# Two matmuls of 256 tokens in place of one of 512 in the weight-slot products of a hybrid transformer stack

## The chip, the cores and the metric

The kernel runs on one core of one Trainium2 chip. The metric is the device time of one execution in microseconds (us), taken as the median over the runs. The names of the engines are those of the profile: PE is TensorE's matmuls, PEld its weight loads, DVE is VectorE, ACT is ScalarE, POOL is GpSimd, and SP is SyncE, which issues the DMAs.

## The reference, cut to what matters

One block of mixed attention and convolution is followed by four layers of another block (mLSTM, sliding-window attention, HGRN2, differential attention). There are 512 tokens, the model width is 1024, the hidden width of every feed-forward part is 2816, and everything is in float32. What the change touches is the dense products: the input projections, the output projections and the feed-forward matrices.

```python
x = x + groups @ w_out
h2 = rms_norm(x, g_ffn)
return x + (jax.nn.silu(h2 @ w_gate) * (h2 @ w_up)) @ w_down      # first block
...
gu = h @ w_in                                                      # layers 0 to 3
return (jax.nn.silu(gu[..., :FFN_HIDDEN]) * gu[..., FFN_HIDDEN:]) @ w_out
```

## The kernel before, in words

Activations lie feature-major in SBUF: 128 features on the partitions, the 512 tokens along the free axis, so an activation of width 1024 is 8 chunks of 128x512, and the hidden one of width 2816 is 22. Each float32 product is made of three products of the one-pass format fp32r: the weight and the activation are each split into a high and a low part, and high x high, high x low and low x high are added in PSUM. The parts are `w_hi`, `w_lo`, `h_hi`, `h_lo`, `hid_hi` and `hid_lo`.

The weights come as a stream of 501 slots of 128x1024 values (512 KB). SP loads a slot into one of four buffers `raw`, ACT copies it to `w_hi` (L1440), POOL subtracts to `w_lo` (L623), and PE uses it. A slot is eight 128x128 weight blocks.

On PE a slot is used in one of several ways:

- `slot_products` (from L750), called by `m_tile`, takes the weights as the stationary operand and moves 128x512 activations past them. For each of the slot's blocks it issues three matmuls, L756, L757 and L758, all into one bank of PSUM, 128 outputs by 512 tokens. L756 and L757 have the same weights `w_hi`. One tile of a projection of width 1024 is one slot (24 matmuls); one of the down projection is three slots with 8, 8 and 6 blocks. Each call begins with a wait for the slot's low part (L752). `linear` calls `m_tile` in a loop of four tiles, so of 96 matmuls, wherever at least four tiles are left; `residual_tiles` calls it for the output and down projections without a loop.
- `early_chunk` (L854, L855, L859) does the first three tiles after a norm chunk by chunk, `gate_piece` (L1258 to L1260) does the output gates of two layers, and `value_slot` (L808 to L810) and `value_tile` (L825 to L827) make token-major values with the activations as the stationary operand. `mlstm_gates` (L1245 to L1247) and the compressed blocks of the first part (L1153) are small products of the same format. None of these is touched.

Each matmul call becomes two instructions, a weight load (LDWEIGHTS, PEld) and a MATMUL (PE). The banks are read out by ACT and DVE, whose signals `lin_free` let PE reuse one of four banks.

Of the kernel before, what the change touches and what calls it, by code (L numbers as in the profile page):

```python
# [218 lines left out]
def program(nc, xT, wstream, ada, cond, cols, kept, bigc, layerc, pos, yT, parts):  # L219
    slots_total = stream_length(parts)  # L220
    ctx = ExitStack()
    with ctx:
# [4 lines left out]
        def place(name, shape, dt, at=None):  # L227
            size = int(np.prod(shape[1:]))
            if at is None:
                at = top[0]  # L230
                top[0] += -(-size // 8) * 8
            return nc.alloc_sbuf_tensor_at(name, shape, dt, offset=base + 4 * at)
# [9 lines left out]
        w_hi = [place(f"w_hi{r}", [P, 8, P], F32R) for r in range(RING)]  # L242
        w_lo = [place(f"w_lo{r}", [P, 8, P], F32R) for r in range(RING)]
# [68 lines left out]
        for lv in range(7):  # L312
            b, at = 2 << lv, big + 40 * S if lv == 0 else ada_at + 2048 - (4096 >> lv)
# [432 lines left out]
        def _(pe):  # L746
            n = Counts()
            mm, turn = nc.tensor.matmul, nc.tensor.transpose

            def slot_products(k, i, step, pairs, first, last):  # L750

                pe.wait_ge(sm.lo_done, k + 1 + step * i)  # L752
                r = k % RING
                for at, (out, w, hi, lo) in enumerate(pairs):
                    begin, end = first and w == 0, last and w == len(pairs) - 1
                    mm(out, w_hi[r][:, at, :], hi, start=first and at == 0, stop=False)  # L756
                    mm(out, w_hi[r][:, at, :], lo, start=False, stop=False)  # L757
                    op = mm(out, w_lo[r][:, at, :], hi, start=False, stop=last and at == len(pairs) - 1)  # L758
                op.then_inc(sm.slot_used, 1)

            def m_tile(k, mt, i, step, mt_step, hi, lo, chunks, parts_from=None):

                if mt >= 4:
                    pe.wait_ge(sm.lin_free, mt - 3 + mt_step * i)
                c0 = 0
                for s, m in enumerate(chunks):
                    if parts_from is not None:
                        pe.wait_ge(sm.part_lo, parts_from + c0 + m)
                    slot_products(k + s, i, step,
                                  [(bank[mt % 4][:, 0:hi.shape[2]], c, hi[:, c0 + c, :], lo[:, c0 + c, :])  # L770
                                   for c in range(m)], s == 0, s == len(chunks) - 1)
                    c0 += m
# [2052 lines left out]
```

## Time and profile before

| | before |
|---|---|
| median of 2 runs | 3290.38 us (3289.63 to 3291.13) |
| span of the profiled execution | 3288.7 us |
| PE busy | 3220.8 us, 98% |
| PEld busy | 2619.6 us, 80% |
| DVE, ACT, POOL busy | 1549.8, 1202.1, 1480.9 us |
| matmuls, and as many weight loads | 15181 |
| HBM traffic | 114 GB/s over the span |

The span is the time from the first to the last instruction of one execution. PE's busy time is the union of its matmuls, which overlap: a matmul's record runs until its results are written, while the next has started long before. What one matmul costs in a stream is therefore the distance between two starts, not its duration. The profile was taken on the only core.

### The profile page before, as it was taken

Reading aid. Unit: us, or ns where it says so; the run is one execution under the profiler, and the core shown is the slowest. Engines: PE = TensorE matmul, PEld = TensorE weight load, DVE = VectorE, ACT = ScalarE, POOL = GpSimd, SP = SyncE. Lnnn points to the kernel's source line nnn. Section 1 sums busy time; section 2 is a strip of 40 time slices with the busy share of each in tenths; the row PEclk is TensorE's granted clock in tenths of the full one; section 3 lists DMA queues with packets and bytes.
Section 4 is the critical chain, followed back from the end, with each engine's and each line's share of the span. In section 5 each row is a group of like instructions: output and inputs, shape, how many; then the busy total and the mean of one; then the engine's idle time right before and its main releaser. Section 6 shows DMA issues by size and latency. Waiting matters only on the chain.

```text
span 3288.7 us, 42736 instructions
## 1 busy us (share of the span) xinstructions
PE 3220.8 (98%) x15181; PEld 2619.6 (80%) x15181; DVE 1549.8 (47%) x2615; ACT 1202.1 (37%) x1875; POOL 1480.9 (45%) x724
## 2 busy tenths in 40 slices
PE   8999999999999999999999999999999999999998
PEld 6876788888778888887888878877888877788886
DVE  2453355501145555467555224656556354752223
ACT  3455333222335332455432243125332243553322
POOL 3540554454235445524544454446444453154442
PEclk9999999999999999999999999999999999999999
DMA  4400155532224554211556333113555322032331
GB/s 161 122 26 1 65 204 191 202 106 93 68 65 160 193 202 145 84 59 63 180 191 208 105 96 96 39 33 103 204 191 188 103 90 77 5 99 96 96 103 64
DMA packets 103107, 376.12 MB, mean 114 GB/s; under 512 B 11456, under 2 KB 11584, under 8 KB 102848
## 3 DMA queue, kind: packets, MB, share of 16 engines
q1 hardware_dynamic: 102816, 373.86, 34.1%
q8 instruction: 81, 1.33, 0.2%
q0 software_dynamic: 160, 0.52, 0.1%
q14 instruction: 50, 0.41, 0.0%
HBM read 372.24 MB, written 2.10 MB: 114 GB/s over the span
## 4 chain that ended last, share of the span: by engine, by line
PE 52%; DVE 2%; ACT 1%; issue 1%; POOL 0%; DVEq 0%; ACTq 0%
PE bank L758 13%; PE bank L757 13%; PE bank L756 13%; PE bank L1362 2%; PE bank L859 1%; PE bank L854 1%; PE bank L855 1%; PE bank L808 1%; PE bank L809 1%; PE bank L810 1%; PE bank L1072 1%; PE bank L1328 1%; PE bank L1089 0%; PE bank L974 0%; PE bank L1258 0%
## 5 line engine op out<-in xcount | busy, mean ns | idle before, releaser
L623 POOL TENSOR_TENSOR w_lo<-raw,w_hi 128x1024 fp32r<-128x1024 f32 x501 | 1227.3, 2455 | 1368.2 <-ACT w_hi L1440 1368.0
L1440 ACT ACTIVATE w_hi<-raw 128x1024 fp32r<-128x1024 f32 x501 | 526.8, 1057 | 1183.2 <-PE bank L758 1022.4
L756 PE MATMUL bank<-h_hi,w_hi 128*128 128x512 f32 x2280 | 889.3, 390 | 0.0
L758 PE MATMUL bank<-h_hi,w_lo 128*128 128x512 f32 x2280 | 887.1, 389 | 0.0
L757 PE MATMUL bank<-h_lo,w_hi 128*128 128x512 f32 x2280 | 887.0, 389 | 0.0
L756 PEld LDWEIGHTS bank<-h_hi,w_hi 128*128 128x128 f32 x2280 | 427.9, 188 | 90.6 <-issue 2.0
L757 PEld LDWEIGHTS bank<-h_lo,w_hi 128*128 128x128 f32 x2280 | 427.9, 188 | 89.7 <-issue 1.0
L758 PEld LDWEIGHTS bank<-h_hi,w_lo 128*128 128x128 f32 x2280 | 427.9, 188 | 89.2
L2608 DVE CUSTOM_DVE_ANT_0 ada_raw<-ada_raw,cond_row 128x1024 f32<-128x1024 f32 x192 | 304.2, 1587 | 280.5 <-DMA ada_raw<-ada 270.6
L756 PE MATMUL bank<-hid_hi,w_hi 128*128 128x512 f32 x880 | 344.0, 391 | 0.0
L758 PE MATMUL bank<-hid_hi,w_lo 128*128 128x512 f32 x880 | 342.4, 389 | 0.0
L757 PE MATMUL bank<-hid_lo,w_hi 128*128 128x512 f32 x880 | 342.4, 389 | 0.0
L2624 DVE TENSOR_TENSOR hid_lo<-layer_const,hid_hi 128x512 f32 (+1 forms) x110 | 228.0, 2073 | 108.5 <-ACT hid_hi L1805 108.5
L661 POOL TENSOR_TENSOR h_lo<-proj,h_hi 128x512 fp32r<-128x512 f32 x40 | 55.7, 1407 | 308.5 <-ACT h_hi L1472 308.5
L757 PEld LDWEIGHTS bank<-hid_lo,w_hi 128*128 128x128 f32 x880 | 165.2, 188 | 35.3 <-issue 1.0
L756 PEld LDWEIGHTS bank<-hid_hi,w_hi 128*128 128x128 f32 x880 | 165.2, 188 | 35.1 <-issue 1.0
L758 PEld LDWEIGHTS bank<-hid_hi,w_lo 128*128 128x128 f32 x880 | 165.2, 188 | 34.3
L1800 ACT ACTIVATE layer_const<-bank 128x512 f32<-128x512 f32 x110 | 65.7, 597 | 321.1 <-PE bank L758 317.0
L2062 DVE SCALAR_TENSOR_TENSOR x<-bank,mod,x 128x512 f32<-128x512 f32 x64 | 48.0, 750 | 264.4 <-PE bank L758 255.7
L2621 DVE TENSOR_TENSOR layer_const<-bank,layer_const 128x512 f32<-128x512 f32 x110 | 75.9, 690 | 201.0 <-PE bank L758 163.4
L854 PE MATMUL bank<-h_hi,w_hi 128*128 128x512 f32 x336 | 135.5, 403 | 1.3 <-ACT h_hi L1472 1.0
L855 PE MATMUL bank<-h_hi,w_lo 128*128 128x512 f32 x336 | 131.9, 393 | 0.0
(411 smaller groups left out, 4016.5 us busy)
## 6 DMA issues: line engine op xcount, KB each, us to landing
raw<-weights SPq DMA_DIRECT2D x501, 512.0 KB, 3.5
ada_raw<-ada SPq DMA_DIRECT2D x192, 512.0 KB, 4.3
layer_const<-layer_const SPq DMA_DIRECT2D x5, 512.0 KB, 3.6
x<-x_t SPq DMA_DIRECT2D x1, 2048.0 KB, 7.5
cond_row<-cond SPq DMA_DIRECT2D x4, 512.0 KB, 4.2
y_t<-x SPq DMA_DIRECT2D x8, 256.0 KB, 2.0
tables<-big_const SPq DMA_DIRECT2D x1, 768.0 KB, 5.9
cols<-columns SPq DMA_DIRECT2D x1, 569.5 KB, 8.4
```

What stands on the lines that cost most here:

```text
L623: nc.gpsimd.tensor_tensor(w_lo[k % RING][:, :, :], raw[k % RING][:, :, :], w_hi[k % RING][:, :, :].bitcast(F32), ALU.subtract).then_inc(sm ...
L756: mm(out, w_hi[r][:, at, :], hi, start=first and at == 0, stop=False)
L757: mm(out, w_hi[r][:, at, :], lo, start=False, stop=False)
L758: op = mm(out, w_lo[r][:, at, :], hi, start=False, stop=last and at == len(pairs) - 1)
L854: mm(out, w_hi[r][:, c, :], h_hi[:, c, :], start=c == 0, stop=False)
L855: mm(out, w_lo[r][:, c, :], h_hi[:, c, :], start=False, stop=False)
L1362: op = mm(bank[3 + m % 3][:, j * P:(j + 1) * P], kk[:, j * P:(j + 1) * P], qq[:, j * P:(j + 1) * P], start=True, stop=True)
L1440: fn(w_hi[t % RING][:, :, :], raw[t % RING][:, :, :], ACT.Copy).then_inc(sm.hi_done, 1)
L1800: fn(sil[q % 2], bank[(mt + 2 * q) % 4][:, :], ACT.Silu).then_inc(sm.sil_done, 1)
L2608: v.tensor_tensor_reduce(w, w, cond_row[:, :], 1.0, 0.0, ALU.mult, ALU.add, ada_part[:, kc:kc + 1]).then_inc(sm.ada_used, 1)
L2621: v.tensor_tensor(sil[q % 2], bank[(mt + 2 * q + 1) % 4][:, :], sil[q % 2], ALU.mult).then_inc(sm.lin_free, 2)
L2624: v.tensor_tensor(hid_lo[:, q + 4 * i, :], sil[q % 2], hid_hi[:, q + 4 * i, :].bitcast(F32), ALU.subtract).then_inc(sm.part_lo, 1)
```

## The change

In `slot_products` each of the three products of a block is made as two matmuls, one for tokens 0 to 255 and one for tokens 256 to 511, with the same weight block and into the two halves of the same bank. The order is: both halves of high x high, both halves of high weights x low activations, both halves of low weights x high activations. Only the very first matmul of a tile has the start flag. The signal that a slot is used is still on the last matmul.

```diff
                 for at, (out, w, hi, lo) in enumerate(pairs):
                     begin, end = first and w == 0, last and w == len(pairs) - 1
-                    mm(out, w_hi[r][:, at, :], hi, start=first and at == 0, stop=False)
-                    mm(out, w_hi[r][:, at, :], lo, start=False, stop=False)
-                    op = mm(out, w_lo[r][:, at, :], hi, start=False, stop=last and at == len(pairs) - 1)
+                    cols = hi.shape[1]
+                    spans = (slice(0, cols // 2), slice(cols // 2, cols))
+                    for w_part, moving, e in ((w_hi, hi, 0), (w_hi, lo, 1), (w_lo, hi, 2)):
+                        for u, span in enumerate(spans):
+                            op = mm(out[:, span], w_part[r][:, at, :], moving[:, span],
+                                    start=first and at + e + u == 0,
+                                    stop=last and at == len(pairs) - 1 and e == 2, skip_group_check=True)
                 op.then_inc(sm.slot_used, 1)
```

## Rows read from the trace of the kernel before

**Rows 1.** The page, parts 1 and 2: busy us (share of span), and PE's clock.
```profile
PE 3220.8 (98%) x15181; PEld 2619.6 (80%) x15181; DVE 1549.8 (47%) x2615; ACT 1202.1 (37%) x1875; POOL 1480.9 (45%) x724
PEclk9999999999999999999999999999999999999999
```
**Rows 2.** Who waited for whom, PE's own waits: us in total, times, longest.
```profile
PE bank L926 <- ACT sq L1821: 12.0, 2, 10.9
PE bank L1079 <- DVE df_p L2224: 8.9, 9, 1.4
```
**Rows 3.** Groups of instructions: xcount | busy us, mean ns of one | idle before.
```profile
L756 PE MATMUL bank<-h_hi,w_hi 128*128 128x512 f32 x2280 | 889.3, 390 | 0.0
L756 PE MATMUL bank<-hid_hi,w_hi 128*128 128x512 f32 x880 | 344.0, 391 | 0.0
L757 PEld LDWEIGHTS bank<-h_lo,w_hi 128*128 128x128 f32 x2280 | 427.9, 188 | 89.7 <-issue 1.0
```
**Rows 4.** Timeline of PE and PEld in a feed-forward loop: start us, us, instruction.
```profile
431.07 0.39 PE L756 MATMUL bank<-h_hi,w_hi 128*128 128x512 f32 x1
431.07 0.19 PEld L757 LDWEIGHTS bank<-h_lo,w_hi 128*128 128x128 f32 x1
...
452.83 0.39 PE L756 MATMUL bank<-h_hi,w_hi 128*128 128x512 f32 x1
```
**Rows 5.** Timeline of PE, the compressed blocks: 256 columns, load of 64.
```profile
131.20 0.28 PE L1153 MATMUL bank<-w_hi,blk_parts 128*64 128x256 f32 x1
...
131.55 0.28 PE L1153 MATMUL bank<-w_lo,blk_parts 128*64 128x256 f32 x1
...
132.00 0.28 PE L1153 MATMUL bank<-w_lo,blk_parts 128*64 128x256 f32 x1
```
**Rows 6.** Timeline of PE, the mLSTM gates: 512 columns, load of 36.
```profile
772.43 0.39 PE L1245 MATMUL bank<-h_hi,ml_gw 128*36 128x512 f32 x1
...
777.95 0.40 PE L756 MATMUL bank<-h_hi,w_hi 128*128 128x512 f32 x1
```
**Rows 7.** Timeline of PEld, value tile of layer 1: loads of 128, 128 moving columns.
```profile
1422.83 0.19 PEld L826 LDWEIGHTS bank<-w_lo,h_hi 128*128 128x128 f32 x1
...
1423.95 0.19 PEld L827 LDWEIGHTS bank<-w_hi,h_lo 128*128 128x128 f32 x1
```
**Rows 8.** The chain that ended last: start us, us, what (float32 passes, two per matmul).
```profile
1533.41 0.86 PE bank L891 x2
...
2074.92 1.78 PE bank L1362 x16
```
**Rows 9.** Line 199 (the loops): PE's queue; all of it, then from 409 us.
```profile
L199 PEldq COMPARE_BRANCH  x63: 76/207/240, 72.8 to 3138.9; - x63
L199 PEldq MOVE  x10: 29/29/29, 51.0 to 2921.2; - x10
...
L199 PEldq MOVE  x1: 29/29/29, 409.3 to 409.3; - x1
```
**Rows 10.** Timeline of PE where that loop's first matmul starts.
```profile
412.71 0.84 PE L859 MATMUL bank<-h_lo,w_hi 128*128 128x512 f32 x3
413.39 0.39 PE L756 MATMUL bank<-h_hi,w_hi 128*128 128x512 f32 x1
```
**Rows 11.** DMA queues, instructions: 52 to 56 us, then 72 to 117 us (packets, MB).
```profile
q8 instruction: 1, 0.02, 1.6%
...
q14 instruction: 1, 0.01, 0.1%
```
**Rows 12.** The page: making the low and high weights, loading a slot.
```profile
L623 POOL TENSOR_TENSOR w_lo<-raw,w_hi 128x1024 fp32r<-128x1024 f32 x501 | 1227.3, 2455 | 1368.2 <-ACT w_hi L1440 1368.0
L1440 ACT ACTIVATE w_hi<-raw 128x1024 fp32r<-128x1024 f32 x501 | 526.8, 1057 | 1183.2 <-PE bank L758 1022.4
raw<-weights SPq DMA_DIRECT2D x501, 512.0 KB, 3.5
...
y_t<-x SPq DMA_DIRECT2D x8, 256.0 KB, 2.0
```

## The prediction

> **What bounds the kernel now.** I read the page first. PE is busy 98% of the span at the full clock, 2.4 GHz, and the other engines less than half [rows 1]. Next come PE's own waits: the longest sum is 12.0 us, at the start of the program, the second 8.9 us [rows 2]. So nothing feeds PE late, and the time is what its instructions take one after another. The groups by line then say which instructions. L756 stands with 2280 and 880 matmuls, and L757 and L758 have the same counts, so the changed lines issue 3 x 3160 = 9480 matmuls of 512 columns [rows 3]. Each has a weight load of its own, L757 too, whose weights are already those of L756 [rows 3].
>
> What one costs is the distance of two starts in the timeline. In a feed-forward loop the first matmul of one round starts at 431.07 and that of the next at 452.83 us, and a round is 96 matmuls: 21.76 / 96 = 226.7 ns each [rows 4]. All 9480 take 2149 us, 65% of the span. The load of the next matmul starts together with the present one [rows 4], and the 227 ns hide it.
>
> **The change, part by part.** It removes 9480 matmuls of 512 columns with their loads, and adds 18960 of 256 columns with 18960 loads. The instructions of PE go from 2 x 15181 to 2 x 24661. Nothing moves to another engine or queue, no wait is added, and the columns streamed stay the same. Three things decide: what a half costs in the array, whether its load still hides, and whether PE's queue delivers twice as many instructions.
>
> *The half in the array.* The trace has this format with 256 columns: the compressed blocks. From the fourth matmul of a run to the eighth the starts go from 131.55 to 132.00, 0.45 / 4 = 113 ns [rows 5]. That is half of 226.7 (113.3). From the first to the fourth it is 0.35 / 3 = 117 ns; a restart costs a few ns for its first matmuls. The distance therefore goes with the columns and shows no fixed part, at 0.443 ns per column for both widths. Does the load have a part in the 226.7 ns? No: with a load of 36 columns in place of 128, 24 matmuls take from 772.43 to 777.95, 230 ns each [rows 6]. So I take 2 x 113.3 = 226.7 ns per product, a difference of 0. The upper bound is the slow row, 2 x 117 = 234 ns.
>
> The Trainium skill says otherwise (TensorE: Matmul & The Clock Gate, section "Wait — 56ns, not 53.3ns?"): a matmul takes its columns at 2.4 GHz plus about 2.5 ns, whatever its length. By it 9480 more matmuls would add 23.7 us, an estimate from that page, for 3314 us. The page would also put one of 512 columns at 216 ns, where this trace has 227; so I go by the rows.
>
> *The load.* In the value tile the moving operand has only 128 columns, and ten loads of 128 columns start in 1.12 us: 112 ns each [rows 7]. With the array's part half as long as that, this is the pace of the loads. Now a half gives its load 113.3 ns, and the load wants 112. It hides, with 1 ns to spare. Do load and matmul cost more when they are about equally long? The float32 passes show that case: two of 512 columns take 0.86 us, 0.84 ns per column, so one of 128 columns takes 107 ns in the array; with a load of 112 ns beside it, 16 of them take 1.78 us, 111 ns each [rows 8]. The longer one sets the pace and the other adds nothing. But there the moving operand is read at half the rate. A load running without pause beside a moving operand at full rate stands nowhere in this trace. Bounds: 113.3 ns if nothing is added, and for the upper end the 117 ns of [rows 5], a row with a load of 64 columns, so that the true price could lie above. I take 113.3, because the near-equal case of [rows 8] is the nearest.
>
> *The queue.* PE's sequencer enters the feed-forward loop at 409.3 us [rows 9], and that loop's first matmul starts at 413.39 [rows 10]. The queue is thus filled 4.1 us ahead, 18 matmuls with their loads. With halves the same 36 instructions are worth 18 x 113.3 = 2.0 us. The branch at the loop's end takes 0.21 us [rows 9] and stays covered. In the value tile the sequencer supplied 96 pairs at 112 ns, five times what was queued, in code without a branch [rows 7]. The other side, a sequencer that just keeps that pace, would add its branch to each round that it cannot win back: 51 x 0.21 = 11 us. I take 0.
>
> The branches number 63, of which 10 leave their loop (one MOVE enters each) [rows 9]. Of the 53 taken, 2 lie in loops over values. The rest, 51, are in the changed loops: nine in each of five feed-forward parts and two in each of three input projections.
>
> *The code.* A round is now 4 x 48 = 192 loads and matmuls, and becomes 384. Code comes in by DMA while the kernel runs. In the loop that is entered at 51.0 us one instruction packet arrives in the first round, between 52 and 56 us, 16 KB by the page's rounding of 0.02 MB. In the rounds from 72 to 117 us no packet of that queue is seen, only one of another [rows 11]. The loop goes back over the place where code was fetched, and nothing is fetched again; so the buffer keeps code that lies behind. Whether it keeps 384 instructions and more is not shown. I take 0 and price the miss as a rival.
>
> *Other engines.* They see the same tiles at the same times, since a slot's last half ends where its one matmul ended. A slot needs 1.1 us of ACT and 2.5 us of POOL [rows 12], and PE uses one in 24 x 0.227 = 5.4 us. That does not change.
>
> **Sum.** Against its own time, 3288.7 us of span: array 0, loads 0, queue 0, code 0. What little can only be lost (restarts at 117 in place of 113, loads with 1 ns to spare) I put at about 1 to 2 us. The span becomes 3290, and the measured time lies 1.7 us above the span before (3290.38 against 3288.7): 3292 us.
>
> **Rivals.** A difference of 2%, about what a measurement of this kernel can tell from no change, is 66 us, so 3356 or 3225 us.
>
> *The load no longer hides.* For: a margin of 1 ns, a state the trace does not have, and 117 ns in [rows 5]. Against: [rows 8], and no effect of the load's width at 512 columns [rows 6]. At 117 ns a half it costs 18960 x 3.7 = 70 us: 3362. It decides from 113.3 + 66 / 18.96 = 116.8 ns on. This is the rival on the other side, slower. Chance 0.13.
>
> *Code is fetched again in each round.* The Trainium skill has the rule (Runtime: NRT & Kernel Launch, section "Instruction fetch mechanics"): a taken branch whose target is outside a window of two pages must wait for a DMA; the same section gives PE a larger memory than the others. Worked out from rows, for this kernel: a DMA takes 2.0 us to land for the output and 3.5 us for a slot [rows 12]; the queue covers 2.0 - 0.2 = 1.8 us. So 0.2 to 1.7 us would be lost on each of 51 branches, 10 to 87 us, and twice that fetch if two pieces are wanted. The loss decides from 66 / 51 = 1.3 us a branch. Against: the loop of [rows 11] that goes back without a fetch. Chance 0.10, of which 0.06 is over 2%.
>
> *A small loss:* a few ns on a product from any cause above, for 3300 to 3325 us. Chance 0.15.
>
> *A half needs less than half in the array:* then loads at 112 ns would set the pace: 9480 x (224 - 226.7) = -26 us, 3266. [Rows 5] speak against it. Chance 0.03. That the second half loads nothing, because its weights are there, would save only loads that are hidden, and L757 shows that they are not left out [rows 3]. For a gain of over 2% I have no mechanism; 0.02 is left for it, and 0.02 for an unknown loss of over 2%.
>
> **How the numbers follow.** The forecast, no change, has 0.55. Faster: 0.02. Slower: 0.13 + 0.06 + 0.02 = 0.21. Within 2%: 0.55 + 0.04 + 0.15 + 0.03 = 0.77. The range has to keep 8 in 10: from 3284, just below the forecast, to 3362, the time at 117 ns. Outside lie the gain, the loads as the bound, and the upper parts of the first two rivals. The likeliest case alone is 3288 to 3300.
>
> **What would show it.** Right: 24661 matmuls and loads; halves whose starts lie 113 ns apart in the loops; durations of about 277 ns; no more idle time of PE; clock unchanged. The load as the bound shows as starts above 114 ns everywhere, each load starting after, not with, its matmul. The code rival shows as gaps of PE every 21.8 us in the feed-forward loops, put down to issue, with packets on q8 in every round. The queue rival shows as the same gaps without packets. The forecast is wrong if a half costs over 116.8 ns.

## The result

The changed kernel takes 3418.66 us (two runs, 3418.37 to 3418.95) against 3290.38 us: 1.039 times the time before, 95% interval 1.036 to 1.042, or 128 us more. The forecast was 3292 us in a range from 3284 to 3362 us. The result lies above that range, and none of the rivals had the right cause.

The page of the changed kernel, part 1, answers to [rows 1], and who waited for whom on PE (us in total, times, longest) to [rows 2]:

```profile
PE 3349.1 (98%) x24661; PEld 3121.1 (91%) x24661; DVE 1551.3 (45%) x2615; ACT 1202.2 (35%) x1875; POOL 1475.6 (43%) x724
```

```profile
PE bank L930 <- ACT sq L1825: 12.5, 2, 11.4
PE bank L1083 <- DVE df_p L2228: 8.9, 9, 1.4
```

PE has the 24661 matmuls and loads that were foreseen, is busy as before, and waits as little as before. The span grew from 3288.7 to 3417.2 us with nothing waiting for anything new: a half takes more than half of the old distance.

The groups by line (xcount | busy us, mean ns of one | idle before), then the timeline of PE in a feed-forward part, and the timeline of PEld just before it (start us, us, instruction):

```profile
L760 PE MATMUL bank<-h_hi,w_hi 128*128 128x256 f32 x4560 | 920.9, 283 | 0.0
...
L760 PEld LDWEIGHTS bank<-h_hi,w_lo 128*128 128x128 f32 x4560 | 711.2, 192 | 0.0
```

```profile
424.76 0.40 PE L760 MATMUL bank<-h_hi,w_lo 128*128 128x256 f32 x2
...
426.92 0.40 PE L760 MATMUL bank<-h_hi,w_lo 128*128 128x256 f32 x2
```

```profile
424.64 0.31 PEld L760 LDWEIGHTS bank<-h_hi,w_lo 128*128 128x128 f32 x2
424.88 0.31 PEld L760 LDWEIGHTS bank<-h_hi,w_hi 128*128 128x128 f32 x2
```

Each row of the timeline merges two halves, and such a row starts every 0.24 us. From 424.76 to 426.92 lie 18 halves: 2.16 / 18 = 120.0 ns each, and 240.0 ns for a product where it was 226.7 [rows 4]. The duration of one half is 283 ns, where 277 was foreseen. The blocks' row had promised 113 [rows 5]. Over 9480 products the difference is 9480 x 13.3 = 126 us, nearly all of the 128. The forecast's question is thus down to one number: why does a half cost 120 ns and not 113?

The rival about code can be read off without an experiment. Line 199, PE's queue, shows when the first changed loop is entered, and the DMA queues from 51 to 75.5 us and from 75.5 to 123 us show the packets of code (packets, MB):

```profile
L199 PEldq MOVE  x1: 29/29/29, 53.6 to 53.6; - x1
```

```profile
q8 instruction: 2, 0.03, 0.6%
...
q1 hardware_dynamic: 1152, 4.19, 29.3%
q14 instruction: 1, 0.01, 0.0%
```

The loop of 384 matmuls and loads is entered at 53.6 us. Two packets arrive on q8 in its first round, and none in the two rounds that follow, up to 123 us. Part 3 of the pages of before and after shows the same for the whole program:

```profile
q8 instruction: 81, 1.33, 0.2%
...
q8 instruction: 117, 1.92, 0.2%
```

PE runs 18960 instructions more. 51 x 192 = 9792 of them repeat a round, which leaves 9168 new ones in the code. The 36 packets more hold just these, 255 each. Had each round fetched its code again, there would be about 74 more. The code of the loops is kept, and no branch waits for it.

### The profile page after: what moved, and what is told of

Read it like the earlier page. It is cut to its first block, busy times and chain, and to the rows that moved or that the text cites. A ratio compares the mean times of both kernels' runs of the same rounds, so it can differ in the third digit from the quotient of the medians.

```text
span 3417.2 us, 61696 instructions
## 1 busy us (share of the span) xinstructions
PE 3349.1 (98%) x24661; PEld 3121.1 (91%) x24661; DVE 1551.3 (45%) x2615; ACT 1202.2 (35%) x1875; POOL 1475.6 (43%) x724
## 4 chain that ended last, share of the span: by engine, by line
PE 53%; DVE 2%; issue 0%; ACT 0%; POOL 0%; DVEq 0%; ACTq 0%
PE bank L760 39%; PE bank L1366 2%; PE bank L863 1%; PE bank L858 1%; PE bank L859 1%; PE bank L812 1%; PE bank L814 1%; PE bank L1076 1%; PE bank L813 1%; PE bank L1093 1%; PE bank L1332 0%; PE bank L978 0%; PE bank L1262 0%; PE bank L907 0%; PE bank L1264 0%
## 5 line engine op out<-in xcount | busy, mean ns | idle before, releaser
L1444 ACT ACTIVATE w_hi<-raw 128x1024 fp32r<-128x1024 f32 x501 | 527.1, 1056 | 1291.2 <-PE bank L760 1128.5
L760 PE MATMUL bank<-h_hi,w_hi 128*128 128x256 f32 x4560 | 920.9, 283 | 0.0
L760 PE MATMUL bank<-h_lo,w_hi 128*128 128x256 f32 x4560 | 918.8, 283 | 0.0
L760 PE MATMUL bank<-h_hi,w_lo 128*128 128x256 f32 x4560 | 918.8, 283 | 0.0
L760 PEld LDWEIGHTS bank<-h_hi,w_hi 128*128 128x128 f32 x4560 | 712.3, 192 | 4.2 <-issue 3.0
L760 PEld LDWEIGHTS bank<-h_hi,w_lo 128*128 128x128 f32 x4560 | 711.2, 192 | 0.0
L760 PE MATMUL bank<-hid_hi,w_hi 128*128 128x256 f32 x1760 | 356.2, 284 | 0.0
L760 PE MATMUL bank<-hid_hi,w_lo 128*128 128x256 f32 x1760 | 354.6, 283 | 0.0
L760 PE MATMUL bank<-hid_lo,w_hi 128*128 128x256 f32 x1760 | 354.6, 283 | 0.0
L858 PE MATMUL bank<-h_hi,w_hi 128*128 128x512 f32 x336 | 136.7, 407 | 1.2 <-ACT h_hi L1476 1.0
L859 PE MATMUL bank<-h_hi,w_lo 128*128 128x512 f32 x336 | 132.4, 394 | 0.0
```

The source lines that it names most:

```text
L760: op = mm(out[:, span], w_part[r][:, at, :], moving[:, span], start=first and at + e + u == 0, stop=last and at == len(pairs) - 1 and e == ...
L858: mm(out, w_hi[r][:, c, :], h_hi[:, c, :], start=c == 0, stop=False)
L859: mm(out, w_lo[r][:, c, :], h_hi[:, c, :], start=False, stop=False)
L1444: fn(w_hi[t % RING][:, :, :], raw[t % RING][:, :, :], ACT.Copy).then_inc(sm.hi_done, 1)
```

## The experiments

### Series of matmuls behind the kernel

The kernel before, with 23 series of 48 matmuls behind its last work (cut to the first two), run once:

```diff
                 ffn(None if part == "first" else pivot(sums_down[0]))
                 if part != "first":
                     layer_norm(sums_down[0], sums_down[2])
+            pe.wait_ge(sm.lin_free, n["mt"])
+            for c in range(48):
+                mm(bank[0][0:128, 0:512], w_hi[0][:, c % 8, 0:128], h_hi[:, c % 8, 0:512], start=True, stop=True)
+            for c in range(48):
+                mm(bank[0][0:96, 0:512], w_hi[0][:, c % 8, 0:96], h_hi[:, c % 8, 0:512], start=True, stop=True)
...
```

> The kernel before, with 23 series of 48 matmuls each put behind its last work on PE, where the other engines are idle; they write banks that nobody reads, so the output is unchanged. Read is the distance of two starts in each series, by columns streamed / columns loaded. The trace of after has 120.0 ns for 256/128 in place of the 113.3 that I took from 256/64. Theory A: a matmul of this format takes its columns at 2.4 GHz (106.7 ns for 256) and a part that goes with the columns loaded, 13.3 ns for 128: 512/128 227 ns, 512/64 220, 512/32 217, 384/128 173, 320/128 147, 256/128 120, 256/64 113, 256/32 110, 128/64 60. Theory A': the fixed part is 13.3 ns whatever is loaded, and 256/64 in the trace of before is something else: 512/x 227, 256/x 120. Theory B: the columns cost 0.443 ns each without a fixed part, and a load that runs without pause is slowed to 120 ns: 512/x 227, 384/128 170, 320/128 142, 256/128 120, 256/64 and 256/32 113. For 192/128 and 128/128 all say the pace of the load, 112 to 120 ns. The same weights in pairs, halves of one bank or of two banks: 120 ns in each for A; lower in two banks if the bank is what costs. Float32 passes: 430, 216 and 112 ns for 512, 256 and 128. All of it adds about 270 us.

The chain that ended last (start us, us, what) gives each series in one row:

```profile
3276.70 10.91 PE bank L1424 x48
3287.61 11.04 PE bank L1426 x48
3298.65 11.03 PE bank L1428 x48
3309.68 10.88 PE bank L1430 x48
3320.56 11.12 PE bank L1432 x48
3331.68 8.33 PE bank L1434 x48
3340.01 7.03 PE bank L1436 x48
3347.05 5.75 PE bank L1438 x48
3352.80 5.57 PE bank L1440 x48
3358.37 5.45 PE bank L1442 x48
3363.82 5.44 PE bank L1444 x48
3369.26 5.34 PE bank L1446 x48
...
3378.85 5.33 PE bank L1450 x48
3384.18 2.88 PE bank L1452 x48
...
3389.95 5.80 PE bank L1456 x48
3395.75 5.76 PE bank L1458 x48
3401.51 41.20 PE bank L1460 x96
3442.71 20.72 PE bank L1462 x96
3463.43 10.72 PE bank L1464 x96
```

Each time is divided by the number of matmuls; for float32 the rows count passes, two to a matmul. The last column is what is left over the columns. In fp32r the times of 512 and 256 columns late in their series, 226.7 and 120.0 ns, differ by 106.7, which is 0.4167 ns a column, one cycle at 2.4 GHz; a float32 pass takes two cycles a column (429 to 216 ns):

| line | columns moved / loaded | ns each | over the columns |
|---|---|---|---|
| L1424, L1434, L1436, L1438 | 512, 384, 320, 256 / 128 | 227, 173.5, 146.5, 119.8 | 14, 13.5, 13, 13 |
| L1446, L1450 | 192, 128 / 128 | 111.3, 111.0 | the load sets the pace |
| L1426, L1428, L1430, L1432 | 512 / 96, 64, 36, 32 | 230, 230, 227, 232 | 17, 17, 13, 18 |
| L1440, L1442, L1444 | 256 / 96, 64, 32 | 116.0, 113.5, 113.3 | 9, 7, 7 |
| L1452 | 128 / 64 | 60 | 7 |
| L1456, L1458 | 256 / 128, same weights in pairs: halves of one bank, two banks | 120.8, 120 | 14, 13 |
| L1460, L1462, L1464 | float32 passes, 512, 256, 128 / 128 | 429, 216, 112 | 2.5, 2.5, load |

The first two lines settle it. With 128 columns loaded, a matmul costs its columns at 2.4 GHz and 13.3 ns more, and it does so at every length from 256 to 512 (226.7, 173.3, 146.7 and 120.0 ns in the second half of each series, when its start is over). At 384 and 320 columns the load has 60 and 35 ns of room, so this is no load that comes too late: theory B, with 142 ns for 320 columns, falls. Nor is it the bank, the repeated weights, or other engines' traffic, which are absent here.

With 256 columns the part shrinks with the load's width, 13, 9, 7, 7 ns for 128, 96, 64, 32. The blocks [rows 5] load 64, and that is why they showed 113. But theory A, a part proportional to the width, falls at 512 columns, where narrower loads cost as much or more. So does A', which has no place for 113.5. The exact law for narrow loads stays open; the kernel's matmuls all load 128. The series added 203 us in all; the 270 of the expectation was a wrong addition and tells nothing.

### One product of three in halves

```diff
                     mm(out, w_hi[r][:, at, :], hi, start=first and at == 0, stop=False)
-                    mm(out, w_hi[r][:, at, :], lo, start=False, stop=False)
+                    for span in (slice(0, 256), slice(256, 512)):
+                        mm(out[:, span], w_hi[r][:, at, :], lo[:, span], start=False, stop=False, skip_group_check=True)
                     op = mm(out, w_lo[r][:, at, :], hi, start=False, stop=last and at == len(pairs) - 1)
```

> Only the middle one of the three products (high weights x low activations) is made as two halves, 3160 products of 9480; the two others stay one matmul of 512 columns. A fixed part of 13.3 ns per matmul (theories A and A') adds 3160 x 13.3 = 42 us: 3332 us. Theory B, in which only loads that follow each other without pause are slow, has a long matmul before and behind each pair, so its loads have time: 113.3 to 116 ns a half, 0 to 17 us, 3290 to 3307 us.

Measured: 3337.97 us against 3289.84, ratio 1.015 (1.0133 to 1.0167), 48 us more (44 to 55). A loss appears although every pair of halves has long matmuls around it, so loads that follow each other without pause are not needed for it. Per added matmul it is 15.2 ns, a little over the 13.3. The timeline of PE of this kernel shows where:

```profile
499.86 0.40 PE L759 MATMUL bank<-h_hi,w_lo 128*128 128x512 f32 x1
500.09 0.39 PE L756 MATMUL bank<-h_hi,w_hi 128*128 128x512 f32 x1
500.32 0.40 PE L758 MATMUL bank<-h_lo,w_hi 128*128 128x256 f32 x2
500.55 0.40 PE L759 MATMUL bank<-h_hi,w_lo 128*128 128x512 f32 x1
```

From one L759 to the next, four matmuls take 0.69 us here and 0.697 in the mean of nine such rounds; the columns alone take 640 ns, which leaves about 14 ns for each. Among mixed lengths the part is up to a nanosecond larger.

### Halves in the down projections alone

`slot_products` makes halves only where its caller finds the hidden activation as the moving operand, 2640 products in stretches without a loop.

```diff
+                    if halves:
+                        for w_part, moving, e in ((w_hi, hi, 0), (w_hi, lo, 1), (w_lo, hi, 2)):
+                            for u, span in enumerate((slice(0, 256), slice(256, 512))):
+                                op = mm(out[:, span], w_part[r][:, at, :], moving[:, span],
...
+                        continue
```

> Halves only in the down projections (hidden activations), 880 x 3 = 2640 products of 9480; each is one unbroken stretch of halves. Theory C, 13.3 ns for each added matmul: 35.2 us, 3325 us. The run with one product of three gave 15 ns for each added matmul, because the long matmuls beside the halves became slower too (233 ns for 227); if that is the rule, 40 us, 3330 us. A cause that sits in the loops (branch, code) and not in the matmul would give nothing here, since the down projection has no loop: 3290 us.

Measured: 3326.42 us against 3289.59, ratio 1.0112 (1.0095 to 1.0129), 37 us. That is 14.0 ns for each added matmul, in code without a branch; the interval, 31 to 42 us, holds both 13.3 and 15 ns a matmul. The cause is in the matmuls with their loads, not in the loops.

### Another order of the halves

```diff
-                    for w_part, moving, e in ((w_hi, hi, 0), (w_hi, lo, 1), (w_lo, hi, 2)):
-                        for u, span in enumerate(spans):
+                    for u, span in enumerate(spans):
+                        for w_part, moving, e in ((w_hi, hi, 0), (w_lo, hi, 2), (w_hi, lo, 1)):
...
```

> Equal halves as in the changed kernel, but all three products of the first 256 tokens come before those of the second, and in the order high, low, high weights: matmuls that follow on the same weights are 1 in 6 instead of 4 in 6. If the part of 13.3 ns is paid on every matmul, the time stays 3418 us within 0.3%. If it comes from loading the weights that are already there, only 1 in 6 pays: 18960 x (4/6 - 1/6) x up to 13.3 ns = up to 126 us less, 3292 us.

Measured: 3417.64 us in one run, as the changed kernel within 0.03%. That the same weights are loaded twice in a row costs nothing and saves nothing.

### 320 and 192 columns

```diff
-                    spans = (slice(0, cols // 2), slice(cols // 2, cols))
+                    spans = (slice(0, 320), slice(320, cols))
```

> All three products in two matmuls, but of 320 and 192 columns. If the load of the next matmul can only begin when the present one begins, the piece of 192 columns (93 ns by theory A, 85 by B) waits for a load of 112 ns: A 147 + 112 = 259 ns a product, 303 us more than before, 3593 us; B 142 + 112 to 120 = 254 to 262 ns, 259 to 335 us more. If loads could run ahead of the matmuls by more than one, only the fixed parts count: 240 ns as with equal halves, 3418 us.

Measured: 3595.29 us in one run, 305 us more than before, so 226.7 + 305.5 / 9.48 = 258.9 ns a product. The 259 of theory A fits: 147 for the long piece, and 112, the load's pace, for the short one. Theory B's 254 to 262 would fit too, so this run does not choose between them; it is the series that do. What it excludes is the 240 ns of loads that run ahead by more than one matmul: the next load does not begin before the present matmul, so a long matmul does not help the load of the one after the next.

### A second set of series

The same place, other shapes, run once. Two of the series, the first with one weight block and one moving block, the second in bfloat16:

```diff
+            for c in range(48):
+                mm(bank[0][0:128, 0:256], w_hi[0][:, 0, 0:128], h_hi[:, 0, 0:256], start=True, stop=True)  # BENCH
...
+            for c in range(48):
+                mm(bank[0][0:128, 0:256], kp[:, 0:128].bitcast(mybir.dt.bfloat16)[:, 0:128], kp[:, 0:256].bitcast(mybir.dt.bfloat16)[:, 0:256], start=True, stop=True)  # BENCH
```

> The kernel before with a second set of series of 48 behind its last work, all with 128 columns loaded unless said. The first set gave columns at 2.4 GHz plus 13.3 ns for 512, 384, 320 and 256 columns. Theory C: each matmul of this format with a load of 128 pays 13.3 ns, and the pace of the load (111.7 ns) is the only other bound. It gives 248 columns 116.7 ns, 240 columns 113.3, and from 232 down 111.7. Alternating 512 and 256: 226.7 + 120 = 346.7 ns a pair; 512 and 128: 226.7 + 111.7 = 338.3; 384 and 128: 285.0. If the part comes from loading or reading new addresses, series with one weight block, or with one weight block and one moving block, all the time would fall below 120 (down to 109.2 for 256 columns, as a float32 pass has 2.5 ns over its columns); by C they stay at 226.7 and 120. If it comes from where the moving operand lies, 256 columns out of a weight buffer differ from 120; by C not. Series in bfloat16 ask whether the part belongs to the format: 215.8, 109.2 and 55.8 ns for 512, 256 and 128 columns if a matmul there has the 2.5 ns of a float32 pass, 226.7 and 120 if it is the same for every format that takes a column per cycle.

The chain of this kernel: 248, 240 and 232 columns (L1435 to L1439), one weight block all the time with 512 and 256 columns (L1445, L1447), one moving block too (L1449), 256 columns out of a weight buffer (L1451), and bfloat16 with 512, 256 and 128 columns (L1459 to L1463):

```profile
3335.34 5.57 PE bank L1435 x48
3340.91 5.38 PE bank L1437 x48
3346.29 5.36 PE bank L1439 x48
...
3362.35 10.92 PE bank L1445 x48
3373.27 5.75 PE bank L1447 x48
3379.03 5.76 PE bank L1449 x48
3384.79 5.76 PE bank L1451 x48
...
3418.22 10.38 PE bank L1459 x48
3428.59 5.24 PE bank L1461 x48
3433.83 2.68 PE bank L1463 x48
```

Addresses do not matter: L1445 to L1451 stay at 227.5 and 120 ns. The format does. In bfloat16 the same shapes take 10.38 / 48 = 216.2, 109.2 and 55.8 ns, about 2.5 ns over the columns, as a float32 pass has. So the 13.3 ns belong to fp32r. In bfloat16 the load of 128 columns fits even behind 128 moving columns.

Theory C holds in size and not to the nanosecond: 248 and 240 columns take 116 and 112 ns where it says 116.7 and 113.3. Series that alternate two lengths took, in their steady part, 353.3 ns (512 and 256; C: 346.7), 340.0 (512 and 128; C: 338.3) and 286.7 (384 and 128; C: 285.0), each for a pair. With mixed lengths the part is again larger, as in the kernel with one product of three.

### The kernel in bfloat16, with whole matmuls and with halves

If the part belongs to the format, then in another format the same change costs something else. Both kernels were made with bfloat16 parts; each chunk and each weight buffer begins where it did, with the second half of its place unused.

```diff
-F32R = mybir.dt.float32r
+F32R = mybir.dt.bfloat16
...
-        h_hi = place("h_hi", [P, DT, S], F32R)
+        h_hi = wide_place("h_hi", DT)
...
-                                        w_hi[k % RING][:, :, :].bitcast(F32), ALU.subtract).then_inc(sm.lo_done, 1)
+                                        w_hi[k % RING][:, :, :], ALU.subtract).then_inc(sm.lo_done, 1)
```

> The kernel before (matmuls of 512 columns), but all high and low parts of weights and activations are bfloat16 in place of fp32r; each keeps its place in SBUF, and the products are less exact (about 16 bits of each factor in place of all). The series in bfloat16 took 215.9, 109.1 and 55.8 ns for 512, 256 and 128 columns, where fp32r took 226.7, 120.0 and 111.6. If that holds in the kernel, the 11584 matmuls of 512 columns (9480 in the changed lines, 1008, 672 and 384 in the early tiles, values and gates, 40 small ones) save 10.8 ns each, 125 us, and 96 of 128 columns save 5: 3159 us. If ACT or POOL become slower in writing bfloat16, or PE now waits for slots, less: 3160 to 3290 us. If the 10.8 ns belong to the constant operands of the series and not to the format, nothing changes: 3290 us.

> The changed kernel (two matmuls of 256 tokens) with the same bfloat16 parts. If the cost of the change is the part that each matmul pays beside its columns, and that part is 2.5 ns here in place of 13.3, the halves add 9480 x (2 x 109.13 - 215.87) = 22.7 us to the run with whole matmuls in bfloat16: 3182 us if that is at 3159. If the change costs what it does for another reason (the code twice as long, the queue, the banks), it adds the same 128 us here as in fp32r: 3287 us. The Trainium skill (TensorE: Matmul & The Clock Gate, section 'Wait - 56ns, not 53.3ns?') states about 2.5 ns for each matmul, which would be the 23 us.

Measured: whole matmuls 3149.84 us, ratio to before 0.9573 (0.9557 to 0.9589); halves 3175.10 us, ratio 0.9653 (0.9637 to 0.9669). Both were expected a little longer, at 3159 and 3182 us. The change costs 25 us here (expected 23) where it costs 128 in fp32r. The page, part 1, and the groups by line of the kernel with whole matmuls, then the same two of the kernel with halves:

```profile
PE 3084.6 (98%) x15181; PEld 1574.7 (50%) x15181; DVE 1478.7 (47%) x2615; ACT 1198.6 (38%) x1875; POOL 1327.7 (42%) x724
```

```profile
L761 PE MATMUL bank<-h_hi,w_hi 128*128 128x512 bf16 x2280 | 865.1, 379 | 0.1
```

```profile
PE 3103.4 (98%) x24661; PEld 2495.8 (79%) x24661; DVE 1488.3 (47%) x2615; ACT 1198.6 (38%) x1875; POOL 1327.0 (42%) x724
```

```profile
L765 PE MATMUL bank<-h_hi,w_lo 128*128 128x256 bf16 x4560 | 871.3, 273 | 0.0
```

## Why the prediction was wrong

**What bounds the kernel** was right: PE alone, 9480 products of 226.7 ns, nothing waits. It stayed so after the change.

**The half in the array** is the step that failed. The prediction took 113.3 ns from the only row of this format with 256 columns [rows 5] and concluded that the distance goes with the columns, at 0.443 ns each, without a fixed part. It is 120.0 ns: 0.4167 ns a column and 13.3 ns for each matmul. One length never tells how a price divides between a part per column and one per instruction, and the second length came from a matmul with a load of 64 columns, not of 128. The prediction saw that difference and excused it by [rows 6], where a load of 36 columns changes nothing. The series show why that was no test: at 512 columns the load's width hardly matters (227 to 232 ns), at 256 it does (113.3 to 120).

**The rule that was set aside.** The Trainium skill (TensorE: Matmul & The Clock Gate, section "Wait — 56ns, not 53.3ns?") has a fixed 2.5 ns for each matmul. The prediction dropped it because 512 columns took 227 ns and not 216. The runs show that its form was right and its amount that of another format: bfloat16 and float32 passes have 2.5 ns here, fp32r 13.3. By form and row together, 226.7 - 213.3 = 13.3 ns on 9480 more matmuls, the sum would have been 126 us, against 128 measured. That was the upper end that the range lacked; it used 117 ns, the slow start of a row that was itself no fit. In the forecast's sum the term "array 0" should have been 126. The rival of a small loss, "a few ns on a product", had its place there, with 10 to 35 us of the 128.

**The load** was judged rightly: its pace is 112 ns (series of 192, 128 and 232 columns), and under a half of 120 ns it is hidden. It now runs nearly all the time, PEld 91% for 80%, and is not the bound. But it is not without effect: with 64 columns loaded instead of 128 a half takes 113.3 ns and not 120, so half of the 13.3 ns goes with the width of the load, which [rows 6], at 512 columns, could not show. The rival "the load no longer hides" had the right sign, 0.13 of the chances, and the wrong mechanism: at 320 and 384 columns the same 13.3 ns are paid with ample room for the load. The piece of 192 columns is where that rival is true.

**The queue** was right: 24661 pairs and a branch in each round delay nothing; the halves without a loop cost as much each.

**The code** was right: 36 packets more, and no fetch in the second and third round of the loop that was followed. A round is 394 instructions by the trace and a packet holds 255 of them, and counted from the program's start the eight changed loops begin at such different places that at least one must lie in three packets; none is fetched again. Here the Trainium skill (Runtime: NRT & Kernel Launch, section "Instruction fetch mechanics") would have a branch out of a window of two pages wait for a DMA. The trace does not agree with that for PE; it does not speak against the larger memory that the prediction names from the same section.

**A half needs less than half in the array** (0.03) was wrong in fp32r.

## What to carry to other kernels

A price read from one length of an instruction may lie in its columns or in the instruction; before it is halved, find a second length of the same format with the same weight load, and if there is none, let the range reach to the case that all of the excess is paid per instruction. In fp32r a matmul with 128 columns loaded paid 13.3 ns beside its columns, so 512 columns in one matmul is the cheapest way to make a product, and two of 256 cost 6% more. From about 240 columns down the load sets the pace instead (240 columns took 112.1 ns, 232 took 111.7), and each further matmul costs the full 112 ns.

## What the runs showed of the hardware that was not expected

- The part per matmul depends on the format: 13.3 ns in fp32r, 2.5 ns in bfloat16 and in a float32 pass, all with 128 columns loaded. Why fp32r pays more is open. It is not the bank, the addresses, repeated weights, other engines, the load's lateness or the number of rows (64 rows: 5.75 us for 48 matmuls of 256 columns, 120 ns as well). Whether it is paid by the matmul or by taking over newly loaded weights is open too: in every run each matmul has a load of its own.
- In fp32r with 256 columns the part falls with the columns loaded, 13.3, 9.3, 6.7 and 6.7 ns for 128, 96, 64 and 32. With 512 columns it does not: 13.3, 16.6, 16.7 and 18.3 ns for 128, 96, 64, 32, and 13.3 again for 36 (all from the steady end of each series). No simple rule fits both.
- Matmuls of two lengths in turn cost more than the sum of their own paces: 353.3 ns for 512 and 256 columns, where the two alone take 346.7.
- Taking bfloat16 parts in place of the fp32r ones makes this kernel 4.3% faster, at the price in exactness named above.
